# Layer 2 of a three-layer block: banded attention as one sequence of 32 steps, with the pool branch and its gates computed between the steps, and the pooling moved into the input projection

## The reference, cut to what matters

```python
u = rms_norm(h, norm_mix)
proj = u @ w_in          # 512 pool, 512 q, 128 k, 128 v, 1024 gate of pool, 1024 gate of attention
z_pool, q, k, v, g_pool, g_attn = split(proj)
# group g of 128 channels: centred mean over 2, 4, 8 or 16 tokens minus the token, then 128x128, then a scale
y_pool = multiscale_pool(z_pool, w_pool_group, pool_scale) @ w_pool_branch     # 512 -> 1024
# 8 query heads on 2 key heads of 64; a block of 128 queries sees its own and the two neighbouring key blocks
y_attn = windowed_gqa(q, k, v, sink) @ w_attn_branch                           # 512 -> 1024
merged = sigmoid(g_pool) * y_pool + sigmoid(g_attn) * y_attn
h = h + merged @ w_out
```

## Time and profile before

| | |
|---|---|
| median of 3 runs | 2460.6 us (2457.75 to 2460.69) |
| the profiled execution | 2461.67 us |
| its span in the trace | 2459.9 us |
| PE busy | 2260.1 us, 92% of the span |
| DVE, ACT busy | 1315.0 us (53%), 947.1 us (39%) |

### The profile page before, as it was taken

The page is one execution under the profiler, slowest core; times in us unless marked ns, Lnnn a source line. Parts: engine busy times, 40 slices in busy tenths (PEclk is TensorE's granted clock), DMA queues, the critical chain, the costliest instruction groups (busy, mean ns, idle before and its releaser), DMA issues.

```text
span 2459.9 us, 37782 instructions
## 1 busy us (share of the span) xinstructions
PE 2260.1 (92%) x14874; PEld 1738.1 (71%) x14874; DVE 1315.0 (53%) x2058; ACT 947.1 (39%) x1508; POOL 60.5 (2%) x84
## 2 busy tenths in 40 slices
PE   5989999987899999789998999997877999999997
PEld 3846666675688888467776888884644887888885
DVE  5566777753664645655627646456355334434343
ACT  4563433423542323346645423233244433322222
POOL 0001111110000000000000000000000000000000
PEclk8989999978999999899999999998866999999999
DMA  3300000004132332111211322321100332332321
GB/s 123 102 21 23 17 23 15 6 3 148 58 104 94 101 95 86 35 52 32 64 61 57 106 94 94 94 88 55 68 0 4 98 102 80 108 95 94 103 86 60
DMA packets 53024, 168.80 MB, mean 69 GB/s; under 512 B 6920, under 2 KB 11144, under 8 KB 52768
## 3 DMA queue, kind: packets, MB, share of 16 engines
q1 hardware_dynamic: 52896, 167.00, 21.5%
HBM read 164.88 MB, written 2.10 MB: 68 GB/s over the span
## 4 chain that ended last, share of the span: by engine, by line
PE 82%; DVE 13%; ACT 2%; issue 2%; DMA 0%; SPq 0%; DVEq 0%; ACTq 0%
PE bank L1601 61%; PE bank L1620 2%; PE bank L1670 2%; PE bank L1919 2%; PE bank L2024 1%; PE bank L1753 1%; DVE rstd L936 1%; PE bank L1956 1%; PE bank L1938 1%; PE bank L1734 1%; PE bank L2016 1%; DVE rw_k_inv L1080 1%; PE bank L2038 1%; PE bank L1779 1%; DVE x L954 1%
## 5 line engine op out<-in xcount | busy, mean ns | idle before, releaser
L1601 PE MATMUL bank<-a_hi,w_hi 128*128 128x512 f32 x1488 | 598.3, 402 | 40.1 <-DVE w_lo L930 20.1
L1601 PE MATMUL bank<-a_hi,w_lo 128*128 128x512 f32 x1488 | 583.6, 392 | 0.0
L1601 PE MATMUL bank<-a_lo,w_hi 128*128 128x512 f32 x1488 | 583.3, 392 | 0.0
L930 DVE TENSOR_TENSOR w_lo<-w_raw,w_hi 128x1024 fp32r<-128x1024 f32 (+3 forms) x322 | 361.5, 1124 | 300.4 <-ACT w_hi L513 294.7
L513 ACT ACTIVATE w_hi<-w_raw 128x1024 fp32r<-128x1024 f32 (+3 forms) x322 | 310.6, 970 | 183.6 <-PE bank L1601 179.6
L1601 PEld LDWEIGHTS bank<-a_hi,w_hi 128*128 128x128 f32 x1488 | 281.9, 189 | 119.6 <-issue 38.1
L1601 PEld LDWEIGHTS bank<-a_hi,w_lo 128*128 128x128 f32 x1488 | 282.2, 190 | 63.4 <-issue 6.8
L1601 PEld LDWEIGHTS bank<-a_lo,w_hi 128*128 128x128 f32 x1488 | 282.0, 190 | 59.4
L1601 PE MATMUL bank<-b_hi,w_hi 128*128 128x512 f32 x640 | 260.5, 407 | 20.4 <-DVE b_lo L988 19.9
L1601 PE MATMUL bank<-b_lo,w_hi 128*128 128x512 f32 x640 | 251.1, 392 | 0.0
L1601 PE MATMUL bank<-b_hi,w_lo 128*128 128x512 f32 x640 | 251.1, 392 | 0.0
(11 more groups left out here) (296 smaller groups left out, 2892.8 us busy)
## 6 DMA issues: line engine op xcount, KB each, us to landing
w_raw<-in_f0gu SPq DMA_DIRECT2D x44, 512.0 KB, 3.5
w_raw<-in_f1gu SPq DMA_DIRECT2D x44, 512.0 KB, 3.5
w_raw<-in_f2gu SPq DMA_DIRECT2D x44, 512.0 KB, 3.5
w_raw<-in_f0dn SPq DMA_DIRECT2D x16, 512.0 KB, 3.5
w_raw<-in_f1dn SPq DMA_DIRECT2D x16, 512.0 KB, 3.5
w_raw<-in_mix SPq DMA_DIRECT2D x16, 512.0 KB, 3.6
w_raw<-in_f2dn SPq DMA_DIRECT2D x16, 512.0 KB, 3.5
w_raw<-in_in SPq DMA_DIRECT2D x10, 512.0 KB, 3.4
```

The costliest lines, as they stand in the source:

```text
L930: dve.tensor_tensor(w_lo[r][:, 0:n, :], raw[r][:, 0:n, :], w_hi[r][:, 0:n, :].bitcast(F32), ALU.subtract).then_inc(w_split[r], 1)
L1601: mm = pe.matmul(bank[r][:, :], w[r][:, k, :], a[:, k, :], start=(k == 0 and n == 0), stop=(k == kt - 1 and n == 2))
```

## The change

The pooling moves into `in`. The units are reordered (pool tiles, k, v, then the queries), DVE works out the four deviations while units 4 to 7 are being read, PE does the four products after units 5 to 8, and ACT's copies stand with units 6 to 9.

The attention becomes 32 straight-line steps g = 8 j + t. PE runs the scores three steps ahead, in two banks instead of four. The exponentials are not divided before the transposes any more. The weighted sum puts tokens on the partitions (`o2_tok`), and once per j all eight sums are divided there at once (`output2_scaled`); four transposes (`turn_output2`) bring the result back. The sinks' exponentials are one instruction per j instead of eight.

The `mix` phase is split. The pool gate's 8 units (`gpool`) and the pool branch's 8 units (`bpool`) are put block by block between the steps (`fill2`): 96 blocks over the first 30 steps, 3 or 4 blocks in each, with their weights' preparation, the gate's copies (`gate_logits`), two sigmoids over four tiles each (`gate_sigmoids`) and the products (`gated_pool`). What is left, the attention's gate and branch, is a phase `attn` of 16 units (8 and 4 blocks in turn). All products of the `mix` phase are still computed, in the same number.

```diff
-    out += [("in", 10, (8,) * 4), ("mix", 32, (8, 8, 4, 4)), ("out", 8, (8,) * 4)]
+    out += [("in", 10, (8,) * 4), ("gpool", 8, (8,) * 4), ("bpool", 8, (4,) * 4), ("attn", 16, (8, 4, 8, 4)),
+            ("out", 8, (8,) * 4)]
...
+UNITS2 = [("gpool", u) for u in range(8)] + [("bpool", u) for u in range(8)]
+FILL2 = [(v, k) for v, (name, _) in enumerate(UNITS2) for k in range(KS[name][0])]
+FILL2_STEPS = STEPS2 - 2
+def fill2_before(g):
+    return min(len(FILL2), -(-len(FILL2) * g // FILL2_STEPS))
...
@@ scalar
             def read_in(i, r, c):
                 u = SLOTS * i + r
+                if u >= 6:
+                    pool_copy(u - 6)
+                if u == 9:
+                    act.wait_ge(v2_done, 1)
+                    act.activation(v2n[:, :, :], bank[5][:, :].rearrange("p (c n) -> p c n", c=TT), ACT.Copy)\
+                        .then_inc(v2_ready, 1)
                 act.wait_ge(unit_done[r], c + 1)
...
+            for g in range(STEPS2):
+                j, t = g // 8, g % 8
+                turned_copy2(g)
+                if g + 2 < STEPS2:
+                    exp2(g + 2)
+                if t == 6:
+                    sink_exps(j)
+                if t == 3 and j:
+                    output2_high(j - 1)
+                for v in range(len(UNITS2)):
+                    if fill2_step(v) == g:
+                        ahead_of(high, FLAT.index(("gpool", 0)) + v + LEAD)
+                    if v < 8 and fill2_step(v, True) + 1 == g:
+                        gate_logits(v)
+                        if v % 4 == 3:
+                            gate_sigmoids(v // 4)
...
@@ vector
+            for g in range(STEPS2):
+                j, t = g // 8, g % 8
+                if g + 3 < STEPS2:
+                    biased(g + 3)
+                if t == 4:
+                    sink_logits(j)
+                if t == 1 and j:
+                    output2_scaled(j - 1)
+                if t == 3 and j:
+                    output2_low(j - 1)
+                for v in range(len(UNITS2)):
+                    if fill2_step(v) == g:
+                        ahead_of(low, FLAT.index(("gpool", 0)) + v + LEAD)
+                    if v >= 8 and fill2_step(v, True) + 1 == g:
+                        gated_pool(v)
...
@@ tensor
+            def fill2(g):
+                for v, k in FILL2[fill2_before(g):fill2_before(g + 1)]:
+                    name, u = UNITS2[v]
+                    r, c = unit2(v)
+                    hi, lo = opnd["a"] if v < 8 else yp
+                    if k == 0:
+                        if v == 8:
+                            pe.wait_ge(pool_low, 4)
+                        pe.wait_ge(w_split[r], c + 1)
+                        if v >= 2:
+                            before, n = unit2(v - 2)
+                            pe.wait_ge(bank_free[before], n + 1)
...
+            wait_evacuated(pe, "in")
+            for g in range(3):
+                scores2(g)
+            for g in range(STEPS2):
+                j, t = g // 8, g % 8
+                if g + 3 < STEPS2:
+                    scores2(g + 3)
+                turn_prob2(g)
+                fill2(g)
+                if g:
+                    weighted2(g - 1)
+                if t == 2 and j:
+                    turn_output2(j - 1)
+            weighted2(STEPS2 - 1)
+            wait_evacuated(pe, "bpool")
```

More of the change, by code:

```diff
@@ L117 @@
 KS = {p[0]: p[2] for p in PHASES}
-BY_SLOT = ("mix",)
-STRAIGHT = ("r", "in", "vt", "heads")
+BY_SLOT = ("attn",)
+STRAIGHT = ("r", "in", "vt", "heads", "gpool", "bpool")
 FENCES = ("lora",)
@@ L484, in _ @@
             sp.dma_start(pool_w[:, :, :], dram["pool_w"]).then_inc(pool_loaded, 16)
-            load("mix")
+            for name in ("gpool", "bpool", "attn"):
+                load(name)
             load("out")
@@ L872, in _ @@
             over_units(act, "in", read_in, high)
[L874 to L905, removed]
-                                   ACT.Copy).then_inc(p2t_ready, 1)
-                act.wait_ge(o2_done, j + 1)
-                act.activation(tile(ya[0], j), bank[7][:, :], ACT.Copy).then_inc(ya_high, 1)
@@ L919, in _ @@
+            over_units(act, "attn", gate_attn, high)
             square_units("out", "n_f2", lambda j: x[:, j, :], tag="f2")
@@ L1566, in _, with gated_pool @@
-            over_units(dve, "mix", mix, low)
+            def gated_pool(v):
+                r, c = unit2(v)
+                dve.wait_ge(unit_done[r], c + 1)
+                dve.wait_ge(gate_ready, (v - 8) // 4 + 1)
+                dve.tensor_tensor(m[:, v - 8, :], m[:, v - 8, :], bank[v % 2][:, :], ALU.mult).then_inc(bank_free[r], 1)
+            for g in range(3):
+                biased(g)
+            for g in range(STEPS2):
[13 more added lines that the diff above has]
+                        gated_pool(v)
@@ L1568, in add_out @@
+            over_units(dve, "attn", merge, low)
             def add_out(i, r, c):
@@ L1585, in _, with dense @@
         def _(pe):
-            def dense(name, operand, ready=None, then=None, norm_of=None, norm_in=None):
+            def dense(name, operand, ready=None, then=None, norm_of=None, norm_in=None, inside=None):
                 def body(i, r, c):
@@ L1597, in body @@
                             sum_squares(norm_in, k)
+                        if inside is not None and isinstance(i, int) and i == 0:
+                            inside(r, k)
                         if ready is not None and (r == 0 or name == "lora"):
@@ L2045, in _, with beside_in @@
-            pe.wait_ge(ya_low, 4)
-            pe.wait_ge(pool_low, 4)
-            dense("mix", lambda r: (opnd["a"], opnd["a"], yp, ya)[r])
+            def beside_in(i, r):
+                u = SLOTS * i + r
+                if u == 7:
+                    pe.wait_ge(bank_free[1], START["in"][1] + 2)
+                    for c in range(TT):
+                        mm = pe.transpose(bank[5][:, cols(c)], v2[:, cols(c)], const("ident"))
+                    mm.then_inc(v2_done, 1)
+                if 5 <= u < 9:
+                    g = u - 5
+                    if g == 0:
+                        pe.wait_ge(pool_loaded, 16)
+                    pe.wait_ge(pool_dev, g + 1)
+                    if g >= 2:
+                        pe.wait_ge(pool_tmp, g - 1)
+                    pe.matmul(bank[4 + 2 * (g % 2)][:, :], pool_w[:, g, :], dev2[:, :], start=True, stop=True)\
+                        .then_inc(pool_done, 1)
@@ new lines, in weighted2 @@
+            def weighted2(g):
+                j, t = g // 8, g % 8
+                (lo, hi), p = BLOCKS2[t // 2], t % 2
+                if t == 0:
+                    pe.wait_ge(o2_step, 4 * j)
+                pe.wait_ge(p2t_ready, g + 1)
+                for c in range(hi - lo):
+                    mm = pe.matmul(bank[6][:, cols(t, HEAD)], p2t[g % 2][:, c, :], v2n[:, lo + c, HP[p]],
+                                   start=(c == 0), stop=(c == hi - lo - 1), skip_group_check=True)
+                if t == 7:
+                    mm.then_inc(o2_done, 1)
```

338 lines of the change are left out of this document (192 added, 146 removed).

## The result

The median fell from 2460.4 us (2457.75 to 2460.69, 4 runs, one more than in the table before the change) to 2397.9 us (2394.92 to 2404.28, 4 runs), a ratio of 0.975 with a 95% interval of 0.973 to 0.977. The profiled execution took 2399.1 us at a span of 2397.2 us. That is 62.5 us less. The forecast was 2392, and 2397.9 lies in its range from 2384 to 2412.

The account below looks back on a forecast made before the run. PE was taken as full in `mix`'s dense half, but waiting and slow in pooling and attention. Terms summed to 194.2 us in place of 263.1, 68.9 us less: 2392 us, range 2384 to 2412.

Parts of the forecast that it names:

- pooling in `in`: Inside the input projection: four pooling products at 3.4 us and four transposes at 0.44 us add 3.9 us.
- idle at the seam: Between `in` and the steps: PE idles 3.7 us until ACT has read the last bank.
- first exponential: At the steps' start: first transposes wait for the first exponential; PE's four scores cover all but 0.7 us.
- the steps' own work: The 32 attention steps with dense blocks between: 115.1 us on PE, of which 68.7 us are dense.
- waits in the loop: PE waits among the steps for the sigmoid's bank (1.3 us), `bpool` banks, divisions and last copy: together 3.0 us.
- clock's fall at the seam: After the idle time behind `in`: a fall costs 2 to 4 us, none costs nothing; 2.0 us taken.
- `attn`: Phase behind the steps: 288 matmuls at 0.2269 us plus 0.44 us, 65.8 us.
- price of a step: Each attention step on PE: 3.96 us with three key blocks, 3.44 us with two, 16 of each.
- Rival 1: In the 32 steps: waits between engines lose 0.7 us per step, 22 us, giving 2414 us; chance 0.11.
- Rival 2: Sigmoids between exponentials on ACT are not hidden: 9.9 us less 1.3 counted, 2401 us; chance 0.07 beyond 2400.
- Rival 3: Clock stays low in the steps, up to 2507 us; chance 0.03 slower, 0.01 near no change.
- Rival 4: Less is lost: no clock fall, no late banks, scores at 0.70 us, giving 2386 us; chance 0.06 below 2385.

Follow-up runs that it names:

- e3_rows128: Changed kernel with scores contracting all 128 rows in place of the head's 64, so its output differs: 2390.7 us, ratio 0.970.
- f3_padded: Changed kernel with each head's queries padded with zeros to 128 rows, giving the same values: 2389.2 us, ratio 0.970.
- f4_seam_padded: Changed kernel with zero-padded queries and the read of `in`'s last bank moved ahead of the weights' high part on ACT: 2385.0 us, ratio 0.969.
- g1_half: Changed kernel with 48 of the 96 dense blocks between the steps and the rest behind them: 2402.8 us, ratio 0.976.
- f2_one_table: Changed kernel with exponentials in place of the two gate sigmoids, so ACT loads no table between the steps: 2397.1 us, ratio 0.974.
- e2_apart: Changed kernel with all 96 dense blocks put behind the 32 steps: 2445.0 us, ratio 0.993.
- h2_eighth: Changed kernel with 12 of the 96 dense blocks between the steps and the rest behind them: 2436.2 us, ratio 0.988.
- f1_after_again: The changed kernel run again without an edit, as its group's common measure: 2397.1 us, ratio 0.974 against the kernel before.
- e4_seam: Changed kernel with the read of `in`'s last bank put ahead of the weights' high part on ACT: 2396.1 us, ratio 0.973.

## Why the prediction was right, and where its sum was off

From `in`'s old end on, 194.2 us were forecast in place of 263.1. The changed trace gives 264.0 - 64.7 = 199.3 us (64.7 is 1765.6 - 1700.93, the part up to that end before). Term by term (the steps' own work is what the other terms leave of the 126.2 us):

| term | forecast us | measured us |
|---|---|---|
| pooling in `in` | 3.9 | 4.0 |
| idle at the seam | 3.7 | 3.5 |
| first exponential | 0.7 | 0 (another wait, 0.5) |
| the steps' own work | 115.1 | 121.5 |
| waits in the loop | 3.0 | 2.1 |
| clock's fall at the seam | 2.0 | 2.1 |
| `attn` | 65.8 | 65.7 |

- **The mis-sized term is the price of a step.** The prediction bounded the scores by 0.70 and 0.83 us and chose 0.72, "since the same shape at full clock reads 0.70". That row contracts 100 rows, and the products here 64. They took 0.84 and 0.63 us, the upper bound, and the transposes behind them 0.48 and 0.37 in place of 0.33 and 0.22, for which the forecast had no bound at all. Scores, 32 times: 23.5 - 19.8 = +3.7 us. Transposes, in 29 steps: +4.4. Dense blocks at 2.22 us for 9.6 matmuls in place of 2.29, and the weighted sums, gave back 2.6. That makes 5.5 of the 6.4 us (115.1 to 121.5); 0.9 stay unassigned. e3_rows128 and f3_padded show the cause, for with 128 rows the prices are 0.70, 0.49, 0.33 and 0.22, those of the second layer's rows.
- **The first exponential** was not waited for: in the changed kernel PE's first scores ran at half clock and covered it, and in f4_seam_padded, at full clock, no wait for it shows either. The 0.5 us that were measured are the third score's wait for its bank, which the forecast did not have. That the two numbers are near is luck.
- **Waits.** The total was near, its makeup less so. The 1.3 us behind the second sigmoid did not come. From that step's start (1857.86) the product that frees the bank ended after 8.8 us and not 10.0, of which the shorter sigmoid is 0.5, and PE wanted the bank after 9.8 us and not 8.7, since the steps are longer. The two waits for `gated_pool` (L1625) were 0.5 and 0.7 us against 0.4 each, the division cost 0.2 us, twice and not three times, and the last copy 0.5 us in place of 0.3.
- **The clock at the seam** fell, as chosen between two rows. That the cost was hit within 0.1 us is luck: the second profile of the same kernel has 2.5 us, and f4_seam_padded none. The 2.1 us are the excess over full-clock prices until step 1: blocks 4.12 - 2.77, transposes 0.62 - 0.37, scores 3.46 (0.72 + 2.74) - 2.94.
- **Rival 1** (short waits, 22 us) did not come with 3.2 blocks per step. In g1_half, too, PE's added waits are three long ones for the division (3.4 us together), not one in every step. **Rival 2** (sigmoids not hidden) is excluded by f2_one_table. **Rival 3** (the clock stays low) did not come, and e2_apart and h2_eighth show that it was the right thing to fear: it is what this loop does without its blocks. **Rival 4** failed in all its parts: the clock fell, 2.1 us of waits came, and the scores took 0.84 us and not 0.70.
- **What the forecast did not say** is that the clock is most of the gain. It got its 68.9 us as a difference of two lengths, and that came out within 5.1 us. How the 63.8 us divide it did not say: 13.0 us pooling, 2.9 us running order, 47.9 us blocks.
- 1.1 us of the difference between 2392.8 and the profiled 2399.1 us arose upstream; 5.1 us are the terms above.

## What to carry to other kernels

Where a chain of small products runs at half clock, look first for full-size products that can be put between them, and price the gain as the small work's own full-clock time once over (here 47.7 us, against some 53 us of such work: 23.5 + 13.2 + 16.0 for scores, transposes and weighted sums), not as its waits. A share of the blocks may do (here half brought nine tenths), which leaves the rest free for another thin stretch. Take a matmul's price from a row with the same number of contracted rows and with the same neighbours, or bound it; and look at the instruction behind it too.

## What the runs showed of the hardware

- A float32 product that contracts 64 rows costs 0.14 us more than one over 128 (0.84 against 0.70 us for 384 columns), and the transposes behind it 0.15 us more. Padding with zeros made it cheaper.
- A loop can keep PE busy and still stay at half clock: in e2_apart PE was busy for 98.5 of 105.1 us with scores, transposes and weighted sums alone, at PEclk 0.50. With 48 full-size blocks among the same steps it read 1.00 in nearly all of the loop.
- The clock after a pause: with 3.46 us of idling it was low for some 7 us (the changed kernel, f1_after_again, f2_one_table), with 3.47 us in e3_rows128 and 4.19 in f3_padded for some 3.5 us only, with 0.73 us and short waits behind in e4_seam for some 3.5 us, and with 1.33 us in f4_seam_padded not at all. So the length of the pause alone does not tell how long the clock stays low. f4_seam_padded and e4_seam have nearly the same waits there. What makes the one fall and the other not stays open, with one trace of each.
- Upstream of any change `rstd` started between 1697.2 and 1706.0 us in the fourteen traces. A whole-program time compares kernels here to some 5 us. A stretch between two fixed points repeated within 0.5 us, in the two profiles of the changed kernel and the one of f2_one_table.
